# A two-layer trunk on one core: token rows of the second expert stage fetched by DMA, other fillers between products, and nine weight places to the end of each expert stage

## The reference

```python
def group_moe(h, w_router, router_bias, w_gate, w_up, w_down):
    ...
    gates = jnp.sum(jax.nn.one_hot(idx, N_EXPERTS, dtype=F32) * w[..., None], axis=1)

    def expert(y, p):
        wg, wu, wd, ge = p
        a = jax.nn.silu(t @ wg) * (t @ wu) * ge[:, None].astype(t.dtype)
        return y + a @ wd, None

    y, _ = lax.scan(expert, jnp.zeros_like(t), (w_gate, w_up, w_down, gates.T))
```

## Time and profile before

| | us |
|---|---|
| median of 3 runs | 1442.75 |
| lowest, highest | 1440.75, 1445.83 |
| the profiled execution | 1440.93 |
| its span | 1439.0 |

### The profile page before, as it was taken

How to read it: one execution, slowest core, us unless ns; L and a number is a source line. 1 busy time by engine, 2 the same in 40 slices (tenths; PEclk the granted TensorE clock), 3 DMA queues, 4 the chain that set the end, 5 groups by cost and what they waited for, 6 DMA issues and landing times.

```text
span 1439.0 us, 17852 instructions
## 1 busy us (share of the span) xinstructions
PE 1354.5 (94%) x6816; PEld 768.3 (53%) x6816; DVE 517.8 (36%) x1376; ACT 282.2 (20%) x580; POOL 47.2 (3%) x63
## 2 busy tenths in 40 slices
PE   5899999997998999889999999999998998899997
PEld 2456556555444444447667567576565544444434
DVE  3145355625111111554464653744513311111123
ACT  3143344411010111231120221212111100001013
POOL 1001200000000000100000000100100000000010
PEclk9999999998999999999999999999999899999998
DMA  9967686926999999912323423224534799579891
GB/s 363 322 244 231 224 279 237 380 95 238 392 396 350 398 395 378 388 64 94 117 82 117 146 88 110 95 89 139 182 118 174 254 398 387 190 258 398 324 399 52
DMA packets 162742, 344.83 MB, mean 240 GB/s; under 512 B 5929, under 2 KB 23554, under 8 KB 162626
## 3 DMA queue, kind: packets, MB, share of 16 engines
q1 hardware_dynamic: 150320, 319.19, 60.4%
q10 hardware_dynamic: 9362, 14.37, 2.7%
q0 software_dynamic: 2944, 9.65, 2.5%
HBM read 324.96 MB, written 18.22 MB: 238 GB/s over the span
## 4 chain that ended last, share of the span: by engine, by line
PE 85%; DMA 6%; DVE 4%; ACT 2%; SPq 2%; issue 1%; DVEq 0%; ACTq 0%
PE psum L1089 14%; PE psum L771 11%; PE psum L786 10%; PE psum L808 9%; PE psum L1120 7%; PE psum L986 7%; PE psum L1206 5%; PE psum L937 3%; PE psum L1198 3%; DMA ring<-in_moe_w_up 3%; PE psum L673 2%; PE psum L1031 2%; DMA ring<-in_da_w_qkv 2%; SPq L569 1%; PE psum L1060 1%
## 5 line engine op out<-in xcount | busy, mean ns | idle before, releaser
L771 PE MATMUL psum<-hT,ring 128*128 128x384 f32 x512 | 173.5, 498 | 8.8 <-DMA ring<-in_da_w_qkv 5.9
L1089 PE MATMUL psum<-ring,work 128*64 128x512 f32 x384 | 170.1, 593 | 2.6 <-DMA ring<-in_moe_w_up 2.6
L1090 PE MATMUL psum<-ring,work 128*64 128x512 f32 x384 | 170.2, 594 | 0.0
L771 PEld LDWEIGHTS psum<-hT,ring 128*128 128x128 f32 x512 | 99.0, 195 | 77.4 <-issue 8.3
L808 PE MATMUL psum<-ring,hT 128*128 128x512 f32 x288 | 125.9, 593 | 0.0
L986 PE MATMUL psum<-work 128*128 128x128 f32 x768 | 106.4, 292 | 5.5 <-issue 3.5
L1089 PEld LDWEIGHTS psum<-ring,work 128*64 128x64 f32 x384 | 51.8, 137 | 111.2 <-issue 111.0
L986 PEld LDWEIGHTS psum<-work 128*128 128x128 f32 x768 | 95.0, 200 | 28.2 <-issue 24.0
L1120 PE MATMUL psum<-ring,work 128*64 128x512 f32 x192 | 89.9, 612 | 1.3 <-issue 1.2
L1975 DVE COPY work<-psum 128x512 f32<-128x512 f32 x32 | 22.1, 692 | 191.2 <-PE psum L1121 191.2
L1121 PE MATMUL psum<-ring,work 128*64 128x512 f32 x192 | 90.0, 613 | 0.0
(11 more groups left out here) (338 smaller groups left out, 1810.0 us busy)
## 6 DMA issues: line engine op xcount, KB each, us to landing
ring<-in_w_ada SPq DMA_DIRECT2D x24, 2048.0 KB, 12.4
ring<-in_moe_w_gate SPq DMA_DIRECT2D x24, 2048.0 KB, 13.0
ring<-in_moe_w_up SPq DMA_DIRECT2D x24, 2048.0 KB, 17.4
ring<-in_moe_w_down SPq DMA_DIRECT2D x24, 2048.0 KB, 17.9
ring<-in_da_w_qkv SPq DMA_DIRECT2D x6, 2048.0 KB, 14.8
sq<-in_moe_w_gate SPq DMA_DIRECT2D x8, 1536.0 KB, 12.3
hT<-in_moe_w_up SPq DMA_DIRECT2D x8, 1536.0 KB, 15.0
work<-in_moe_w_down SPq DMA_DIRECT2D x24, 512.0 KB, 11.3
```

The source lines that it names most:

```text
L771: last = mm(b[:, 0:TOK], w[:, kt, col:col + P], hT[:, kt, :], start=kt == 0, stop=kt == KT - 1)
L1089: mm(psum[0:BLK, x, :], xk, wg[kt], start=kt == 0, stop=kt == KT - 1)
L1090: last = mm(psum[BLK:P, x, :], xk, wu[kt], start=kt == 0, stop=kt == KT - 1)
```

## The change

- **Weight places.** `WHOLE` is gone. Units 0 to 38 cycle through the nine places; the last nine units, of experts 13 to 15, take places 6, 7, 8, 3, 4, 5, 0, 1, 2. So the units of expert 13 follow those of expert 11 in the spare places, those of expert 14 follow expert 10, and those of expert 15 follow expert 12. The slots behind the places are numbered anew in both stages and in between, with the same order of loads.
- **Products started early.** In the second stage before every odd expert, and in the first stage before expert 15 alone, the steps kt = 0 and 1 of the next expert's gate and up products stand ahead of the wait for `gated`, and step 2 stands behind the transposes. The side work of expert 15 moves to kt = 4 to 7.
- **Rows fetched.** In the second stage the gather products of pairs 1 to 7 are gone. ScalarE stores the token rows `htok` to `token_rows` in HBM (two DMAs, 1.5 MB in all). For each pair TensorE multiplies `sel` with a column of token numbers (`list_tokens`), VectorE copies the list as integers (`token_list`), GpSimd fetches the 128 rows with an indirect DMA of 0.5 MB into half of `xs` (`row_loads`), and TensorE turns them in eight transposes (`turn_rows`), six before the wait for `gated` of the odd expert and two behind its transposes. `xs` then has one buffer. The list of a pair is made one pair ahead of its transposes. Pair 0 is gathered as before.
- **Start.** The first units of q and k are loaded in two halves of 256 columns each, first halves first; heads 0 and 1 wait for the first halves only.

```diff
@@ constants, plan_units @@
+AHEAD = 3
-    plan = {(e, 2 * i + 1): pair(e - 1, i) for e in range(LAST + 1, NE) for i in range(4)}
+    plan = {(e, AHEAD + 1 + i): pair(e - 1, i) for e in range(LAST + 1, NE) for i in range(4)}
-WHOLE = 3 * (NE - EPG)
-    order = ((2, 3, 0, 1, 4, 5), (4, 5, 2, 3, 0, 1))
+    order = ((2, 3, 0, 1, 4, 5), (4, 5, 1, 2, 3, 0))
-        units.extend(u + (order[0][i % RSLOT],) for i, u in enumerate(rest))
+        units.extend(u + ((1, 2, 3, 0)[i % RSLOT],) for i, u in enumerate(rest))
+        tail = [6, 7, 8, 3, 4, 5, 0, 1, 2]
         for n in range(3 * NE):
-            place = n % wide if n < WHOLE else (n - WHOLE) % NSLOT
+            place = n % wide if n < 3 * NE - wide else tail[n - 3 * NE + wide]
@@ sync @@
                     if name == ("q", 0):
-                        sp.dma_start(att_tab, att_d).then_inc(in_att, 16)
+                        for half in range(2):
+                            for kind in "qk":
+                                here = slice(256 * half, 256 * half + 256)
+                                to, src = source((kind, 0))[0]
+                                sp.dma_start(to[:, :, here], src[:, :, here]).then_inc(slot_full[slot_of[(kind, 0)]] if half else in_first[kind], 16)
+                            if half == 0:
+                                sp.dma_start(att_tab, att_d).then_inc(in_att, 16)
@@ tensor, project @@
-                if i == 0:
+                if h == 0:
+                    pe.wait_ge(in_first[kind], 16)
+                elif h == 2 or i == 0:
                     unit_wait(pe, (kind, g))
@@ tensor, experts @@
+                def list_tokens(q):
+                    pe.wait_ge(m["sel"], q + 1)
+                    if q > 1:
+                        pe.wait_ge(m["listed"], q - 1)
+                    chosen = sel_second if q == 1 else sel
+                    for t in range(TT):
+                        last = mm(psum[:, 4, 0:1], chosen[:, t].rearrange("p x s -> p (x s)"),
+                                  table(base_sb, base_at, "token")[:, t:t + 1], start=t == 0, stop=t == TT - 1)
+                    last.then_inc(m["ids"], 1)
+                def turn_rows(q, kts):
+                    pe.wait_ge(m["rows"], 16 * q)
+                    pe.wait_ge(m["xs"], 2 * q)
+                    for kt in kts:
+                        last = tr(psum[:, 2 + kt // 4, P * (kt % 4):P * (kt % 4) + P], xrow[:, P * kt:P * kt + P], ident)
+                        if kt % 4 == 3:
+                            last.then_inc(m["gathered"], 1)
...
+                            pipelined = lambda n: n % 2 == 1 and (l == 1 or n == NE - 1)
+                            gate_up(e, range(AHEAD if pipelined(e) else 0, KT // 2))
+                            hint = pe.mark_branch_hint_location()
+                            wg, wu = gate_up(e, range(KT // 2, KT))
                             overflow(e, wg, wu, hint)
                             more = q + 1 < NE // 2
-                            if more:
+                            if pipelined(e + 1):
+                                gate_up(e + 1, range(AHEAD - 1))
+                            if more and l == 0:
                                 pe.wait_ge(m["sel"], q + 2)
                                 pe.wait_ge(m["xs"], q * 2 + x + 1)
                                 gather(x, range(4 * x, 4 * x + 3))
+                            if more and l and x:
+                                if q + 2 < NE // 2:
+                                    list_tokens(q + 2)
+                                turn_rows(q + 1, range(6))
                             pe.wait_ge(m["gated"], e + 1)
...
                             side_work((e, "T"))
-                            if more:
+                            if pipelined(e + 1):
+                                gate_up(e + 1, range(AHEAD - 1, AHEAD))
+                            if more and l == 0:
                                 gather(x, (4 * x + 3,)).then_inc(m["gathered"], 1)
+                            if more and l and x:
+                                turn_rows(q + 1, range(6, KT))
@@ scalar, experts @@
+                if l:
+                    for half in range(2):
+                        emptied(act, ("htok", l, TT * half + TT - 1))
+                        act.dma_start(token_rows_d.rearrange("(t p) d -> p t d", p=P)[:, :, 512 * half:512 * half + 512],
+                                      htok[:, :, 512 * half:512 * half + 512]).then_inc(m["kept"], 16)
...
-                            if q + 1 < NE // 2:
+                            if q + 1 < NE // 2 and l == 0:
                                 take_xs(q + 1, 1 - par, x)
+                            if q + 1 < NE // 2 and l and x:
+                                take_xs(q + 1, 0, 0)
+                                take_xs(q + 1, 0, 1)
@@ vector, experts @@
+                def token_list(q):
+                    dve.wait_ge(m["ids"], q)
+                    V.tensor_copy(ids[:, q:q + 1], psum[:, 4, 0:1]).then_inc(m["listed"], 1)
@@ gpsimd @@
+            def row_loads():
+                m = M[1]
+                pool.wait_ge(m["kept"], 32)
+                for q in range(1, NE // 2):
+                    pool.wait_ge(m["listed"], q)
+                    if q > 1:
+                        pool.wait_ge(m["gathered"], 2 * q)
+                    pool.indirect_dma_start(out=xrow, out_offset=None, in_=token_rows_d,
+                                            in_offset=bass.IndirectOffsetOnAxis(ap=ids[:, q:q + 1], axis=0)).then_inc(m["rows"], 16)
```

67 lines of the change are left out of this document (45 added, 22 removed).

## The result

The changed kernel took **1462.04 us** (median of 5 runs, 1456.74 to 1470.13), the kernel before 1442.75 (1440.12 to 1445.83): ratio 1.014, 95% interval 1.0106 to 1.0174. I had said 1444, within 1434 to 1453. It is slower by 19 us, and my range did not hold it. The profiled execution took 1470.13 us (span 1468.3). It is the slowest of the five, 8.1 us above their median, with a mean granted clock of 0.962 where the other four had 0.966 to 0.969: what is read from its trace adds up to 29 us over before and not to 19.

The account below looks back on a forecast made before the run. First stage bound by its weight stream, second by TensorE; the last up weights' landing decides. Start -0.5, first stage +11.3, second -8.9 give +1.9 on 1440.93: 1442.8, plus 1.8 for the median 1444.6, stated as 1444, range 1434 to 1453.

Parts of the forecast that it names:

- What bounds the kernel: Both expert stages: the last up weights' landing and work behind it decide; first stage stream-bound, second bound by TensorE.
- Start: Kernel start: halves of q and k win at most 2.1 us, low clock loses 1.7; 0.5 us won taken.
- the size of the low clock: Value products at the start: TensorE's lower clock level after the idle gap loses 1.7 us.
- Places in the first stage: First expert stage: new places make expert 15's up weights land 5.0 us later.
- The stream's dry time: First expert stage: weight stream runs dry at 530.9 and restarts at 534.8, then never stops.
- the half that the gathers take: Stage ends: row gathers take half the bandwidth, so the rest of the last weights comes at half rate.
- Expert 15's early products: First-stage end: expert 14's transposes and down product fall behind the landing, 4.6 us, plus 1.7 us of low clock.
- The second stage, TensorE's part,: Second stage: gather matmuls removed, lists and transposes added; expert 5's transposes move from 1238.1 to 1226.8, expert 7's 1286.6 to 1271.1.
- The second stage, the landing of wu15: Second-stage end: last expert's up weights land 15.2 us earlier; minus 4.6 and 1.7, 8.9 us won.
- Row fetches: Second stage: 0.52 MB fetches, needed over 20 us later, landing in 8.3 to 13.0; hidden, except perhaps the first.
- The rivals: Gathers and fetches ahead, 1451 to 1453 (0.22); second-stage stream less full, about 1438 (0.20); first-stage places work, 1425 to 1430 (0.05).
- Gathers ahead of the last weights: Slower rival, both stage ends: gathers go whole before the last weights, +10, 1451 to 1453 us; chance 0.22.

Follow-up runs that it names:

- e8: Changed kernel with old places, old start and no early products of expert 15, leaving row fetches and second-stage early products up to expert 13: 1453.09 us.
- e10: Changed kernel with old start, no early products of expert 15, and new places in the second stage only, code unshifted: 1448.04 us.
- e9: Kernel before, same work and order, with 6 more TensorE instructions at its very start to shift its code: 1450.69 us, ratio 1.0049.
- e15: Kernel before with the new order of places alone, in both stages, TensorE code the same instruction for instruction: 1457.41 us, ratio 1.0097.
- e5: Changed kernel with TensorE's branch hint at the start of an expert's products instead of their middle: 1462.62 us.
- e1: The changed kernel run again with no edit, for a second profile: 1459.72 us.
- e12: Changed kernel with old start, no early products of expert 15, new places in the second stage only, code shifted by 18 instructions: 1438.53 us, ratio 0.9966.
- e11: Changed kernel with old start, no early products of expert 15, new places in the second stage only, code shifted by 12 instructions: 1441.99 us, ratio 1.0008.
- e4: Changed kernel with q and k fetched whole again (the old start): 1458.34 us.

## Why the prediction was wrong, point by point

**What bounds the kernel** held: the landing of the last up weights and what stands behind it decided both stages.

**Start.** -0.5 forecast, +0.2 measured (75.72 against 75.51), a difference smaller than the scatter of the start (T(0) stands between 356.76 and 359.99 in the seventeen profiles). The mechanism was right, the size of the low clock was not: 2.2 us over the value products in place of 1.7, against 2.0 won ahead of them. That the changed kernel's profile stands 2.8 us behind at T(0) is not the halves: e8 and e10, with the old start, stand there too, and e9, with no change at all, 2.0.

**Places in the first stage.** Forecast 5.0 us, measured 6.3 (alone) and 6.4 (whole change, shifted). The stream's dry time, 3.9 against 4.1, was right, and so was the half that the gathers take: from 579.2 to 587.2 in e15 their queue moved 1.65 MB and that of the weights 1.58. What the sum lacked are the units queued behind wu15. From the restart at 533.78 to the landing at 587.22 the weight queue moved 17.78 MB, and its 8 units are 16.78; in before, from 547.36 to 580.42, it moved 11.58 for 10.49. So about 1 MB of later units goes ahead of wu15's last bytes in both; at half the rate it costs more than at the full one, which can make the 1.3 us.

**Expert 15's early products.** Forecast 6.3 us, measured 7.6 in the run without a pause at T(15), e5, counted from the landing (20.83 against 13.22), and 5.0 as the difference between two runs with one. Right within 1.3.

**The step that failed in the first stage is one that the sum doesn't have**: what TensorE's code costs by its place. My sum read TensorE's lead as unchanged up to T(11). In all eight profiles of the changed kernel and its unshifted variants there was a pause of 3.2 to 3.6 us at expert 3; at the end of the stream it made 3.7 us in e1 (10.0 against 6.4) and 2.1 to 5.3 in the other four profiles with the new places, and a late fetch at T(15) 1.3 to 2.0 more (8.9 and 9.6 from the landing on against 7.6). The shares of pause and places don't simply add: the pauses alone made 10.0 us in e9, the places alone 6.3 in e15, and both together 10.0 in e1. I had the row before me: the 2.50 us pause in expert 11. I used it only as something that a full stream would hide, and not as something that any edit of TensorE's code can move to where nothing hides it.

**The second stage, TensorE's part,** was right where no pause fell. T(5) came 11.0 us earlier than before relative to the stage in e12 (forecast 11.3), T(7) 13.9 (forecast 15.5). In the changed kernel itself T(7) came 5.6 earlier: the pause of 3.10 us at expert 0 with the low clock behind it took 5.0 (its T(0) came 4.9 later, in e12 0.1 earlier), and of the remaining 3.3 two are idle rows of 1.0 us with the releaser "issue".

**The second stage, the landing of wu15, is the step that failed by most.** Forecast 15.2 us earlier. Measured with the new places and without a pause at expert 0: 9.1, 10.5 and 11.9; with one, 4.1 to 8.1, in the changed kernel's first profile 5.0. Behind it stands the cost of expert 15's early products, 6.3 us by forecast and 7.0 in that profile and in the run shifted by 16, and so the stage won nothing: 8.9 forecast, 0.2 measured in the shifted run and 2.0 lost up to T(15) in the first profile. Two errors, both of this one term: the pause, some 4 us, and 3.3 to 6.1 us that the stream lost against my sum without any pause. In e12, where it lost 3.3, 1.6 of them are T(7)'s. For the rest a candidate stands in its queues: from the restart at 1283.37 to the landing at 1391.45 the weight queue moved 37.16 MB where my 17 units are 35.65. The 1.5 MB of units behind wu15 are 3.8 us at 396 GB/s, but before's sum lacks as much of the same kind (11.08 MB for 10.49 from 1360.55 to 1392.74, 1.5 us), so at most 2.3 us of the miss can be this.

**Row fetches** were hidden, as forecast: the list of waits has no wait for them, and their median landing was 8.6 us.

**The rivals.** None was the right one. Gathers ahead of the last weights, my slower one, did not happen: they took half. I had given the second stage alone the power to go either way, and had no case with both stages behind.

In sum, for the changed kernel's profile: 29.3 us behind before at the end. 2.8 at T(0); 11.6 to wu15 (6.4 by the run without the pause, the rest with the pause at expert 3 and what followed); 9.2 from there to T(15) (6.3 early products, the rest mostly the late fetch); 3.5 between T(15) and the second stage, of which 1.5 to the one-column products after the first stage, and the rest not looked into; 2.0 in the second stage. The forecast for the same points: -0.5, 5.0, 6.3, 0, -8.9. The largest part of the miss is the last, 10.9 us of 27. This profile is of the slowest of the five executions; the medians are 19.3 us apart, and which of these parts shrinks in the other executions no trace shows.

**What stays open.** Which branch gets a late fetch. Two kernels with the same places modulo 256 agreed (expert 3 in the changed kernel and in before shifted by 6; none there in the two forms shifted by 16 and 18), but a shift by 24 moved the pause by six experts and not one, the pause at expert 0 of the second stage came or stayed away within one kernel's code (it was absent with the old places, where TensorE's code is the same), and an early hint removed one of three. Nor is it shown why the last weights' gain in the second stage varies so much with the same places: with the old ones it was 0.4 us with a pause at expert 0 and 5.8 without, with the new 4.1 to 8.1 and 9.1 to 11.9. Nor what delays the packet at expert 15 by 2.8 and 3.7 us in e11 and e12.

## What to carry to other kernels

Where a weight stream bounds a stage, moving a buffer's release to an earlier or later step is worth what the stream's dry time says and nothing of what the names say; work out when the stream runs dry, with the releaser's time beside it. Don't put work that waits for the last transfer ahead of work that could run meanwhile. And a kernel with branches over long blocks has a time that depends on where its code lies: before an edit is judged by a per cent, compare it at two or three shifts of the code, and read the idle rows whose releaser is "issue" in both traces.

## What the runs showed of the hardware

- Six instructions more on TensorE at the very start cost the kernel before 8 us (1450.69 against 1442.31). One and the same work took 1448.04, 1441.99 and 1438.53 us at three places of its code.
- A fetch of 16.4 KB of instructions occupies a DMA engine for 1.1 us (2.0% of 16 engines' 3.45 us). TensorE stood for much longer: the packet began 0.6 to 1.0 us behind the branch, and work 1.5 to 1.7 us behind its end, 3.2 to 3.6 us in all at expert 3. With the queues otherwise empty (4 GB/s) it was no less, 3.65 us in the changed kernel's pause at expert 15. In e12 it was 6.4 us, the packet beginning 3.7 us after TensorE's last work.
- Behind a pause of 3.3 us the clock cost 0 to 1.9 us more: 18 gather matmuls took 4.18 us at a granted 0.50, 2.28 without a pause, and 2.25 behind the pause of 3.31 us in e4. 48 value products after 6.56 us of idleness took 22.97 us and not 20.76.
